# The last half down projection of a two-layer encoder with tokens as rows, and the final norm taken row by row

## What is computed

```python
def _rmsnorm(x, g):
    x32 = x.astype(jnp.float32)
    y = x32 * lax.rsqrt(jnp.mean(x32 * x32, axis=-1, keepdims=True) + EPS)
    return (y * g.astype(jnp.float32)).astype(x.dtype)

def _swiglu(h, w_gu, w_down):
    g, u = jnp.split(h @ w_gu, 2, axis=-1)
    return (jax.nn.silu(g) * u) @ w_down
...
        h = h + _swiglu(_rmsnorm(h, norm_ffn[i]), ffn_w_gu[i], ffn_w_down[i]).astype(h.dtype)
    return _rmsnorm(h, final_norm)
```

## Time and profile before

| | |
|---|---|
| time, median of 3 runs | 1253.87 us |
| the profiled execution | 1254.49 us |
| its span, first to last instruction | 1252.7 us |
| busy: PE | 1189.5 us, 95% |
| busy: VectorE (DVE) | 629.6 us, 50% |
| busy: GpSimd (POOL) | 403.1 us, 32% |
| busy: ScalarE (ACT) | 354.1 us, 28% |
| mean granted clock of TensorE | 0.987 |

### The profile page before, as it was taken

How to read it: one execution, slowest core, us unless ns; L and a number is a source line. 1 busy time by engine, 2 the same in 40 slices (tenths; PEclk the granted TensorE clock), 3 DMA queues, 4 the chain that set the end, 5 groups by cost and what they waited for, 6 DMA issues and landing times.

```text
span 1252.7 us, 18266 instructions
## 1 busy us (share of the span) xinstructions
PE 1189.5 (95%) x5796; PEld 981.0 (78%) x5796; DVE 629.6 (50%) x1067; ACT 354.1 (28%) x689; POOL 403.1 (32%) x423
## 2 busy tenths in 40 slices
PE   6899989999999999999889899899999999999996
PEld 5777778788888888888867777678788888888885
DVE  5677765433333534454576766745443433343332
ACT  4166652222200111111365665632222200111101
POOL 3333335333321332343241422324333311323342
PEclk8999999999999999999989999999999999999998
DMA  6211103323432333432200101013333332333421
GB/s 161 68 35 35 35 17 105 97 84 100 119 93 75 100 101 91 118 93 89 71 20 18 34 2 33 18 34 118 86 99 100 103 106 77 101 92 92 118 84 67
DMA packets 176475, 96.67 MB, mean 77 GB/s; under 512 B 8752, under 2 KB 173104, under 8 KB 176432
## 3 DMA queue, kind: packets, MB, share of 16 engines
q1 hardware_dynamic: 176432, 96.12, 26.3%
HBM read 94.01 MB, written 2.10 MB: 77 GB/s over the span
## 4 chain that ended last, share of the span: by engine, by line
PE 82%; DVE 8%; issue 4%; ACT 3%; POOL 2%; DMA 1%; ACTq 0%; POOLq 0%; DVEq 0%; SPq 0%
PE bank L953 26%; PE bank L955 25%; PE bank L954 25%; PE bank L1395 2%; PE bank L1084 1%; DVE w_lo L1477 1%; POOL w_hi L442 1%; DVE stat L2008 1%; PE bank L1096 1%; DVE apt_lo L1670 1%; DVE bpt_lo L2013 1%; ACT s_b L884 1%; DMA x_n<-in_x 1%; DVE s_a L1662 1%; DVE k_dup L1588 0%
## 5 line engine op out<-in xcount | busy, mean ns | idle before, releaser
L1477 DVE TENSOR_TENSOR w_lo<-w_raw,w_hi 128x1024 fp32r<-128x1024 f32 (+2 forms) x151 | 202.2, 1339 | 298.6 <-POOL w_hi L442 298.6
L953 PE MATMUL bank<-x_hi,w_lo 128*128 128x512 f32 x784 | 310.7, 396 | 10.2 <-DVE w_lo L1477 8.0
L442 POOL TENSOR_SCALAR w_hi<-w_raw 128x1024 fp32r<-128x1024 f32 (+3 forms) x159 | 183.4, 1154 | 422.5 <-PE bank L955 411.2
L955 PE MATMUL bank<-x_hi,w_hi 128*128 128x512 f32 x784 | 306.8, 391 | 0.0
L954 PE MATMUL bank<-x_lo,w_hi 128*128 128x512 f32 x784 | 306.7, 391 | 0.0
L953 PEld LDWEIGHTS bank<-x_hi,w_lo 128*128 128x128 f32 x784 | 148.2, 189 | 45.7 <-issue 6.3
L955 PEld LDWEIGHTS bank<-x_hi,w_hi 128*128 128x128 f32 x784 | 148.0, 189 | 31.5
L954 PEld LDWEIGHTS bank<-x_lo,w_hi 128*128 128x128 f32 x784 | 148.4, 189 | 29.5
L953 PE MATMUL bank<-f_hi,w_lo 128*128 128x512 f32 x352 | 137.8, 391 | 1.0 <-DVE f_lo L1780 1.0
L955 PE MATMUL bank<-f_hi,w_hi 128*128 128x512 f32 x352 | 137.1, 389 | 0.0
L954 PE MATMUL bank<-f_lo,w_hi 128*128 128x512 f32 x352 | 137.0, 389 | 0.0
(11 more groups left out here) (220 smaller groups left out, 1839.0 us busy)
## 6 DMA issues: line engine op xcount, KB each, us to landing
w_raw<-in_ffn_w_gu SPq DMA_DIRECT2D x88, 512.0 KB, 3.8
w_raw<-in_ffn_w_down SPq DMA_DIRECT2D x32, 704.0 KB, 4.5
w_raw<-in_a_w_qkv SPq DMA_DIRECT2D x12, 512.0 KB, 3.7
w_raw<-in_a_w_o SPq DMA_DIRECT2D x8, 512.0 KB, 3.6
w_raw<-in_b_w_o SPq DMA_DIRECT2D x8, 512.0 KB, 3.8
w_raw<-in_b_w_in SPq DMA_DIRECT2D x4, 672.0 KB, 4.0
w_raw<-in_b_w_uq SPq DMA_DIRECT2D x4, 576.0 KB, 4.0
x_n<-in_x SPq DMA_DIRECT2D x4, 512.0 KB, 5.5
```

The lines of the kernel that those rows point to most:

```text
L442: pool.tensor_scalar(split_part(w_hi, s, cols, kv), raw_part(s, cols, kv), 1.0, 1.0, ALU.mult, ALU.mult) \
L953: pe.matmul(o, ll, rh, start=start, stop=False)
L955: return pe.matmul(o, lh, rh, start=False, stop=stop)
L1477: dve.tensor_tensor(split_part(w_lo, s, cols, kv), raw_part(s, cols, kv), f(split_part(w_hi, s, cols, kv)), ALU.subtract) \
```

## The change

The first half of the last down projection stays. In the second half, tokens are the rows of the result: the stationary side of a matmul is f for 128 tokens, the moving side is 512 output features of a weight row block. All 8 banks are open at once, one for each pair of 128 tokens (t) and half of the features, and the loop runs over the 11 inner blocks k, with 24 matmuls per block. Weight blocks are now rows of w_down, 128 by 1024 (W_COLS instead of W_DOWN). Banks 6 and 7 (t = 3) are still read for hid when the loop starts, so blocks 0 and 1 run for t = 0 to 2 first and for t = 3 after that. The ninth block is loaded into a place of its own ahead of the whole layer (held_raw, held_hi, held_lo). The last three blocks are done bank by bank, nine matmuls each, so that the banks end in turn.

h itself is transposed near the start of this half (turn_h, behind the first gate projection), and ScalarE copies it to h_rows. For each bank VectorE adds it to h_rows and takes the squares with their sum over the features; for each 128 tokens it makes 1/rms with ScalarE's root and writes the second half of the features, scaled and times the gain. GpSimd multiplies the first half with the gain, ScalarE scales it. There are eight output transfers of 256 KB. h_fin, the running sum ss of this norm, turn, turned and the sum over partitions are gone.

```diff
-C_END = C_FFN1 + 2 * C_HALF
+C_LAST = C_FFN1 + C_HALF + 2 * HALF
+LAST_RING = HALF - 1
+HELD = HALF - 3
...
+        held_raw, held_hi, held_lo = region(scratch + 24 * 1024, [
+            ("held_raw", [P, D], F32), ("held_hi", [P, D], F32R), ("held_lo", [P, D], F32R)])
+        (h_rows,) = region(scratch + 64 * 1024, [("h_rows", [P, NT, D], F32)])
...
+                    if layer and half:
+                        for r in range(LAST_RING):
+                            k = HALF + (r if r < HELD else r + 1)
+                            load((C_LAST + r) // 2, (C_LAST + r) % 2, last_v[:, k:k + 1, :], D)
+                        continue
...
-            sp.dma_start(g_fin[:], final_norm.rearrange("(k n) -> k n", n=P).partition_broadcast(P)) \
-                .then_inc(gfin_in, 16)
+            sp.dma_start(g_fin[:], final_norm.partition_broadcast(P)).then_inc(gfin_in, 16)
+            sp.dma_start(held_raw[:], last_v[:, HALF + HELD, :]).then_inc(held_in, 16)
...
-                sp.wait_ge(out_ready[t % 2], t // 2 + 1)
-                sp.dma_start(ov[:, t, :], out_n[:, t, :]).then_inc(out_sent, 16)
-            sp.wait_ge(out_sent, 16 * NT)
+                sp.wait_ge(out_ready[1], t + 1)
+                sp.dma_start(ov[:, t, 0:T], out_n[:, t, 0:T]).then_inc(out_sent, 16)
+                sp.wait_ge(out_ready[0], t + 1)
+                sp.dma_start(ov[:, t, T:D], out_n[:, t, T:D]).then_inc(out_sent, 16)
+            sp.wait_ge(out_sent, 16 * 2 * NT)
...
+            def last_down():
+                for r in range(2, LAST_RING):
+                    w_split_hi((C_LAST + r) // 2, (C_LAST + r) % 2, W_COLS)
+                    if r == 2:
+                        pool.wait_ge(held_in, 16)
+                        pool.tensor_scalar(held_hi[:], held_raw[:], 1.0, 1.0, ALU.mult, ALU.mult).then_inc(held_hi_ready, 1)
+                pool.wait_ge(gfin_in, 16)
+                for t in range(NT):
+                    pool.wait_ge(last_sq_ready, 2 * t + 1)
+                    pool.tensor_tensor(out_n[:, t, 0:T], h_rows[:, t, 0:T], g_fin[:, 0:T], ALU.mult).then_inc(last_gain, 1)
...
+            def turn_h():
+                for u in range(2 * NT):
+                    act.wait_ge(h_turned, u + 1)
+                    act.activation(h_rows[:, u // 2, u % 2 * T:(u % 2 + 1) * T], banks[u % 6][:], ACT.Copy) \
+                        .then_inc(h_rows_ready, 1)
...
-            ffn_half(1, 1, norms[4])
-            rms(norms[4])
-            act.wait_ge(rs_n_ready, 5)
-            act.wait_ge(pt_free, T_FIN + KD)
-            for t in (1, 3):
-                act.activation(out_n[:, t, :], out_n[:, t, :], ACT.Copy, scale=rs_n[:, 2 * t:2 * t + 1]) \
-                    .then_inc(out_ready[1], 1)
+            ffn_half(1, 1, None)
+            for t in range(NT):
+                act.wait_ge(last_ms, t + 1)
+                act.activation(ms_n[:, 1, t:t + 1], ms_n[:, 0, t:t + 1], ACT.Sqrt).then_inc(last_rms, 1)
+                act.wait_ge(last_rs, t + 1)
+                act.wait_ge(last_gain, t + 1)
+                act.activation(out_n[:, t, 0:T], out_n[:, t, 0:T], ACT.Copy, scale=rs_n[:, t:t + 1]).then_inc(out_ready[1], 1)
...
+            def turn_h():
+                pe.wait_ge(proj_free, U_FFN1 + C_HALF)
+                for u in range(2 * NT):
+                    if u >= 6:
+                        pe.wait_ge(h_rows_ready, u - 5)
+                    rows = slice(u // 2 * P, (u // 2 + 1) * P)
+                    for m in range(KD // 2):
+                        last = pe.transpose(banks[u % 6][:, m * P:(m + 1) * P], h[:, u % 2 * KD // 2 + m, rows], ident[:])
+                    last.then_inc(h_turned, 1)
+            def last_down(j0):
+                def rows(k, t, hi, lo, halves=(0, 1)):
+                    at = slice(t * P, (t + 1) * P)
+                    for half in halves:
+                        cols = slice(half * T, (half + 1) * T)
+                        last_ = product(banks[2 * t + half][:], f_hi[:, k, at], f_lo[:, k, at], hi[:, cols], lo[:, cols],
+                                        k == 0, k == HALF - 1)
+                    return last_
+                def ring(r):
+                    s = (C_LAST + r) % 2
+                    return w_hi[s], w_lo[s]
+                pe.wait_ge(h_rows_ready, 2 * NT)
+                for k in range(2):
+                    pe.wait_ge(w_ready, C_LAST + k + 1)
+                    pe.wait_ge(f_ready, j0 + k + 1)
+                    for t in range(NT - 1):
+                        rows(k, t, *ring(k))
+                pe.wait_ge(proj_free, U_LAST)
+                for k in range(2):
+                    rows(k, NT - 1, *ring(k)).then_inc(w_used, 1)
+                for k in range(2, HELD):
+                    pe.wait_ge(w_ready, C_LAST + k + 1)
+                    pe.wait_ge(f_ready, j0 + k + 1)
+                    for t in range(NT):
+                        last = rows(k, t, *ring(k))
+                    last.then_inc(w_used, 1)
+                pe.wait_ge(held_ready, 1)
+                pe.wait_ge(w_ready, C_LAST + LAST_RING)
+                pe.wait_ge(f_ready, j0 + HALF)
+                for t in range(NT):
+                    for half in range(2):
+                        rows(HELD, t, held_hi, held_lo, (half,))
+                        rows(HELD + 1, t, *ring(HELD), (half,))
+                        rows(HELD + 2, t, *ring(HELD + 1), (half,)).then_inc(last_done, 1)
...
+                            if fin and j == 0 and s == 0:
+                                turn_h()
...
+                if fin:
+                    last_down(j0)
+                    return
...
-                def turn(m0, s):
-                    pe.wait_ge(proj_free, U_DOWN1 + m0 + s + 1)
-                    pe.wait_ge(pt_free, T_FIN + m0 + s - 1)
-                    for t in range(NT):
-                        last = pe.transpose(banks[3 + s][:, t * P:(t + 1) * P], h_fin[:, s, t * P:(t + 1) * P], ident[:])
-                    last.then_inc(pt_done, 1)
...
-                if fin:
-                    turn(0, 0)
                 with pe.Fori(1, KD // 2) as i:
                     down(i, 0)
-                    if fin:
-                        turn(2 * i - 2, 1)
                     down(i, 1)
-                    if fin:
-                        turn(2 * i, 0)
-                if fin:
-                    turn(KD - 2, 1)
-                    sum_partitions(norms[4])
...
+            def last_down():
+                for r in range(2, LAST_RING):
+                    w_split_lo((C_LAST + r) // 2, (C_LAST + r) % 2, W_COLS)
+                    if r == 2:
+                        dve.wait_ge(held_hi_ready, 1)
+                        dve.tensor_tensor(held_lo[:], held_raw[:], f(held_hi[:]), ALU.subtract).then_inc(held_ready, 1)
+                dve.wait_ge(h_rows_ready, 2 * NT)
+                dve.wait_ge(gfin_in, 16)
+                for t in range(NT):
+                    for half in range(2):
+                        u = 2 * t + half
+                        view = h_rows[:, t, half * T:(half + 1) * T]
+                        dve.wait_ge(last_done, u + 1)
+                        dve.tensor_tensor(view, view, banks[u][:], ALU.add).then_inc(last_sum, 1)
+                        dve.wait_ge(last_sum, u + 1)
+                        dve.tensor_tensor_reduce(last_sq[:, half, :], view, view, 1.0 / D, 0.0, ALU.mult, ALU.add,
+                                                 stat[:, 0, u:u + 1]).then_inc(last_sq_ready, 1)
+                    mean, step, r = ms_n[:, 0, t:t + 1], ms_n[:, 2, t:t + 1], rs_n[:, t:t + 1]
+                    dve.wait_ge(last_sq_ready, 2 * t + 2)
+                    dve.scalar_tensor_tensor(mean, stat[:, 0, 2 * t:2 * t + 1], EPS, stat[:, 0, 2 * t + 1:2 * t + 2],
+                                             ALU.add, ALU.add).then_inc(last_ms, 1)
+                    dve.wait_ge(last_rms, t + 1)
+                    rs_stepped(dve.reciprocal(r, ms_n[:, 1, t:t + 1]))
+                    rs_stepped(dve.tensor_tensor(step, mean, r, ALU.mult))
+                    rs_stepped(dve.scalar_tensor_tensor(step, step, -0.5, r, ALU.mult, ALU.mult))
+                    dve.scalar_tensor_tensor(r, step, 1.5, r, ALU.add, ALU.mult).then_inc(last_rs, 1)
+                    dve.wait_ge(last_rs, t + 1)
+                    dve.scalar_tensor_tensor(out_n[:, t, T:D], h_rows[:, t, T:D], r, g_fin[:, T:D], ALU.mult, ALU.mult) \
+                        .then_inc(out_ready[0], 1)
...
-                hidden(HALF - 1, W_DOWN)
+                hidden(HALF - 1, W_COLS if layer and half else W_DOWN)
+                if layer and half:
+                    last_down()
+                    return
...
-                def turned(m, s):
-                    wait(dve, pt_done, T_FIN + m + 1)
-                    dve.tensor_tensor(out_n_v[:, :, m, :], banks[3 + s][:].rearrange("p (t n) -> p t n", t=NT),
```

(50 more changed lines are left out.)

13 lines of the change are left out of this document (7 added, 6 removed).

## The result

The changed kernel is slower: 1257.43 us, the median of 7 runs (1254.77 to 1259.6), against 1251.73 of 7 runs of the kernel before, measured beside it. The ratio is 1.0038, 95% interval 1.0022 to 1.0054, so 4.8 us (2.8 to 6.8) of 1252. It is the ratio of the means, 1256.88 and 1252.12; the two medians alone stand 5.7 apart. The forecast was +4.7, and 1258.5 in all.

The account below looks back on a forecast made before the run. The prediction took PE, busy 95% of the span, as the bound. Turns 0.7 and stalls 4.8 against a shorter tail gave 2.8 more; clock 1.9 made it 4.7, on a median of 1253.87: 1258.5 us, range 1254.5 to 1262.

Parts of the forecast that it names:

- the clock: Behind PE's two stalls the clock may fall to 1.2 GHz: 1.35 falls of 1.4 us, 1.9 on average.
- A: Stretch from the down projection's first matmul to the start of its last 72: forecast 48.4 us without the clock.
- stalls: PE waits for weights at block 2 (2.1 us) and before the last 72 matmuls (2.7), 4.8 in all.
- B: Stretch from the start of the last 72 matmuls to the end of the span: forecast 26.9 us.
- The turns: 32 transposes of h behind the first gate projection: 3.6 us where 2.9 stood, 0.7 more, no clock fall charged.
- the collision in the first: At PE's first stall, GpSimd's held_hi holds up VectorE's w_lo for block 2: 0.8 us.
- The collision: In the last part, GpSimd's gain product holds up VectorE's squares: 0.5 us per block from the second on.
- the tail: From PE's end to the span's end, shrinking only from 13.3 to 10.6 us as VectorE works off its queue.
- The first (no fall): Rival: all else as forecast, but the clock stays at 2.4 GHz in both stalls; 1256.7 us, chance 0.15.
- The second: Rival: in the last part VectorE keeps pace with PE, at most 4.08 us per block; not slower, chance 0.12.
- The third: Rival: the turns of h lower the clock; 1.7 us on top, 1260.2, chance 0.05.
- the fourth: Rival: swapped operands or bank changes cost matmul pitch in the down projection; 3 us at 5%, 1261.5, chance 0.06.

Follow-up runs that it names:

- e6: Changed kernel with the edits of e1 and e2 together, so neither wait of PE for weights is left: 1248.15 us, 0.9969 of the kernel before.
- e2: Changed kernel with all tokens run from block 0 on, so the first slot comes free after 24 matmuls: 1254.43 us, 1.0009 of the kernel before.
- e1: Changed kernel with the last (eleventh) weight block loaded into a place of its own: 1254.82 us, 1.0015 of the kernel before.
- e5: Changed kernel with the held block split one slot earlier on both engines: a single execution, not timed; first wait 1.2 us.
- e8: The same edit as e5, held block split one slot earlier than in the changed kernel, timed: 1255.39 us, 1.0026 of the kernel before.
- e4: Changed kernel with GpSimd's gain product waiting for both squares of a group: a single execution, not timed; groups 5.2 us apart.
- e7: Changed kernel with e1, e2 and e3, the root's table loaded early and the mean in another form: 1246.67 us, 0.9955 of the kernel before.
- changed, again: The changed kernel measured once more, with no edit: 1256.42 us, 1.0038 of the kernel before.
- e3: Changed kernel with the squares and their sum moved from VectorE to ScalarE: 1258.61 us, 1.0045 of the kernel before.
- e9: The same edit as e4, gain product after both squares, against the changed kernel, timed: 1258.03 us, 1.0044 of the kernel before.

## Why the prediction was right

**The sum.** The mechanism came as forecast, and each of its steps can be measured by itself. Without the clock, A was forecast as 1228.6 - 1180.2 = 48.4: 43.6 of matmuls, 2.1 and 2.7 of stalls. e6 has no stall and takes 43.5; e2 adds the second alone, 2.7; e1 has the first with its fall, 3.9. As the trace counts them, the two waits of the changed kernel are 1.98 and 2.56, forecast 2.0 and 2.5. B was forecast as 1255.5 - 1228.6 = 26.9 and is 26.6 and 26.7 in the kernels whose clock stays up. The turns took 3.4 to the next matmul (forecast 3.6), PE waited for nothing behind them, and they did not lower the clock. For this last the forecast had a weaker ground than it says. The window from 9 to 11 of the kernel before reads 1.00 over transposes, but this one, a little later, reads 1.00 with PE idle for most of it:

```profile
12.00:16.00 4.00, 0.93 (x3) 0.49 (x3) 3.73 (x4) 2.05 (x3) 2.53 (x2) 1.00 0.61 24
```

So the start of the program can't tell transposes from idle time. The turns of the changed kernel can: 3.4 us of them at 1.00, where 1.98 us of idle brought a fall.

**The stalls' causes.** e1 and e2 each took away the one that they were to take away. The share of the collision in the first (0.8) is shown by e5 and e8.

**VectorE as the bound.** 5.25 per group against the forecast 5.3, and gapless but for the root. The collision was sized at 0.5 and is 0.6 (1.28 - 0.69). e4 shows that GpSimd's product was the cause, and not the squares themselves: they take 0.70 there. PE was done 6.9 before VectorE's last product, and from there to the end it was 3.1, both as forecast. The output transfers took 2.2 each (median in e7's page), forecast 2.1.

**The clock was the term with the wrong size.** The forecast charged 1.35 falls of 1.4. In the profiles a fall costs 1.6 to 1.8 (B of the changed kernel against e1's; A of e1 less its wait), and both stalls had one: 3.4 where it took 1.9. The turns and the tail came out 0.2 and 0.3 below their terms, so from the down projection on, the profiles differ by 78.4 - 76.1 + 3.4 of turns = 5.7, and not by 4.7. The runs say 4.8, with an interval of 2.8 to 6.8 in which both lie.

The same sum, A + B + 3.4 - 76.1, can be made for every kernel of the table and set beside its ratio in us: 5.6 and 4.8 (changed, again), 1.3 and 1.9 (e1), 0.3 and 1.1 (e2), -2.6 and -3.9 (e6), 4.7 and 5.6 (e3), -5.7 and -5.6 (e7), 3.2 and 3.3 (e8), 6.1 and 5.5 (e9). They agree within 1.3 us, and the mean of the differences is 0.0. So, by this estimate, the down projection, what follows it and the turns account for the times of all these kernels. The rest of the program is no part of the explanation, though single profiles differ there: before 1176 the clock falls five times in the profile of before, twice in that of after, three to five times in the others. That the forecast came within 0.1 us of the measured difference is luck: its clock term was 1.5 too small, and the measurement isn't that fine.

**The rivals.** The first (no fall) happened once for one of the waits, in e2. The second, VectorE at PE's pace of 4.08, did not come about: 5.25 in the changed kernel, and still 4.22 in e7, with the squares on ScalarE. The third fell with the turns at clock 1.00 and 3.4 us for 32 of them, the fourth with A of 43.5 in e6, a pitch of 0.227.

## What to carry to other kernels

A new order of loops has to be laid against the slots of weights: here two places where PE outran a refill of 2.7 us cost 4.9 us and the lower clock behind them 3.4. That is twice the 3.9 that the new order brings without them (e6); with VectorE relieved too it brings 5.6 (e7). When work is moved to an engine, look at what stands between its steps there (a table load), and at which one-column operations GpSimd still holds up.
